# Expert products by pairs of tokens, and late columns through two output buffers, in a one-core decoder layer on Trainium2

## The reference, cut to what matters

```python
z = rms_norm(x) @ w_in                     # 38 column tiles of 128: 14 "z", 8 "conv", 16 "gate"
z = z + (token_shift(z) - z) * mu          # the 14 z tiles; the first mixer reads them
...
h = u * sigmoid(gate)                      # the 8 conv tiles, by pairs; the second mixer reads them
...
g = sigmoid(z_gate)                        # the 16 gate tiles
h = h + (g_r * o_r + g_c * o_c) @ w_out
# experts: 8 heads x 16 chosen rows = 128 rows of u_tab and 128 of v_tab for each token
coef = gates * gelu(einsum('cd,ced->ce', c, u_tab[idx]))
h = h + einsum('ce,ced->cd', coef, v_tab[idx])
...
```

## Time and profile before

| what | value |
|---|---|
| median of 3 runs | 3401.3 us (3399.88 to 3406.71) |
| the profiled execution | 3405.59 us |
| its span | 3403.9 us |
| granted TensorE clock over the span | 0.89 |
| TensorE busy | 2719.1 us (80%) |
| VectorE busy | 2378.7 us (70%) |
| GpSimd busy | 1978.4 us (58%) |
| ScalarE busy | 525.0 us (15%) |
| moved by DMA | 1248.57 MB, of them 1073.87 MB by the gathers |

### The profile page before, as it was taken

How to read it: one execution, slowest core, us unless ns; L and a number is a source line. 1 busy time by engine, 2 the same in 40 slices (tenths; PEclk the granted TensorE clock), 3 DMA queues, 4 the chain that set the end, 5 groups by cost and what they waited for, 6 DMA issues and landing times.

```text
span 3403.9 us, 41995 instructions
## 1 busy us (share of the span) xinstructions
PE 2719.1 (80%) x15556; PEld 1235.5 (36%) x15556; DVE 2378.7 (70%) x6051; ACT 525.0 (15%) x1166; POOL 1978.4 (58%) x2093
## 2 busy tenths in 40 slices
PE   9988985998989888897867687667766777777787
PEld 7877872333323233233323233232323331222111
DVE  5669898886677765777689877987798747665200
ACT  3221321110121101211010101010111001111101
POOL 1013344665656565566677667776767667666663
PEclk9998996998999999998878887798879788888899
DMA  6558998999999999999999999999999999999995
GB/s 212 197 181 301 334 364 286 373 399 380 371 352 385 390 364 362 340 406 390 410 409 403 405 401 409 397 407 405 400 396 408 406 404 410 409 388 406 410 369 235
DMA packets 385725, 1248.57 MB, mean 367 GB/s; under 512 B 40560, under 2 KB 75120, under 8 KB 384752
## 3 DMA queue, kind: packets, MB, share of 16 engines
q0 software_dynamic: 294912, 1073.87, 81.0%
q1 hardware_dynamic: 90608, 172.01, 14.1%
HBM read 1217.80 MB, written 27.92 MB: 366 GB/s over the span
## 4 chain that ended last, share of the span: by engine, by line
PE 34%; DMA 33%; DVE 16%; POOL 10%; issue 5%; ACT 1%; SPq 1%; POOLq 0%; ACTq 0%; DVEq 0%
DMA e_u<-in_u_tab,e_idx 12%; PE e_acc L1273 8%; DMA e_late<-in_u_tab,e_idx 7%; DMA e_v<-in_v_tab,e_idxT 6%; DVE e_u L2178 5%; PE e_pl L1361 5%; POOL e_v L949 4%; PE e_pd L1156 4%; POOL e_u L941 3%; PE e_acc L1318 3%; PE e_pd L1236 3%; PE e_acc L1343 3%; DVE e_late L2178 2%; PE e_pd L976 2%; DMA shifted_projection<-e_side 2%
## 5 line engine op out<-in xcount | busy, mean ns | idle before, releaser
L2178 DVE CUSTOM_DVE_ANT_0 e_u<-e_u,e_c 128x1024 f32<-128x1024 f32 x776 | 943.3, 1216 | 439.8 <-DMA e_u<-in_u_tab,e_idx 424.4
L941 POOL DMA_INDIRECT e_u<-in_u_tab,e_idx x776 | 757.7, 976 | 651.4 <-DVE e_dots L2178 260.2
L1273 PE MATMUL e_acc<-e_v,e_wd 128*32 128x512 f32 x3096 | 900.5, 675 | 284.5 <-DMA e_v<-in_v_tab,e_idxT 260.6
L949 POOL DMA_INDIRECT e_v<-in_v_tab,e_idxT x774 | 732.8, 947 | 434.7 <-PE e_acc L1273 279.2
L2178 DVE CUSTOM_DVE_ANT_0 e_late<-e_late,e_c 128x1024 f32<-128x1024 f32 x248 | 301.1, 1215 | 132.3 <-DMA e_late<-in_u_tab,e_idx 130.5
L1273 PEld LDWEIGHTS e_acc<-e_v,e_wd 128*32 128x32 f32 x3096 | 122.7, 113 | 736.6 <-DMA e_v<-in_v_tab,e_idxT 493.1
L1361 PE MATMUL e_pl<-e_late,e_v 128*128 128x512 f32 x608 | 342.0, 661 | 54.6 <-DVE e_late L1977 13.5
L1273 PE MATMUL e_acc<-e_late,e_wd 128*32 128x512 f32 x832 | 270.8, 712 | 105.0 <-DMA e_late<-in_v_tab,e_idxT 96.1
L941 POOL DMA_INDIRECT e_late<-in_u_tab,e_idx x248 | 240.5, 970 | 189.8 <-DVE e_dots L2178 148.9
L1906 DVE SCALAR_TENSOR_TENSOR e_gbc<-e_hc,e_cw,e_gbc 128x128 f32<-128x128 f32 x960 | 303.7, 343 | 0.5
L949 POOL DMA_INDIRECT e_late<-in_v_tab,e_idxT x208 | 198.2, 953 | 75.2 <-issue 53.1
(11 more groups left out here) (293 smaller groups left out, 3048.2 us busy)
## 6 DMA issues: line engine op xcount, KB each, us to landing
e_u<-in_w_in SPq DMA_DIRECT2D x38, 512.0 KB, 3.8
e_v<-in_w_in SPq DMA_DIRECT2D x38, 512.0 KB, 6.5
e_v<-in_w_in SPq DMA_DIRECT2D x76, 256.0 KB, 6.4
e_u<-in_u_tab,e_idx POOLq DMA_INDIRECT x776, 9.5
e_v<-in_v_tab,e_idxT POOLq DMA_INDIRECT x774, 9.5
e_zb<-in_w_c SPq DMA_DIRECT2D x48, 256.0 KB, 10.5
e_arena<-in_w_r SPq DMA_DIRECT2D x32, 256.0 KB, 19.8
e_zb<-in_w_r SPq DMA_DIRECT2D x32, 256.0 KB, 6.7
```

The source lines that it names most:

```text
L941: pool.indirect_dma_start(out=rows_in[i], out_offset=None, in_=io["u_tab"], in_offset=bass.IndirectOffsetOnAxis(ap=idx[n % 2][:, j:j + 1], ...
L949: pool.indirect_dma_start(out=rows_in[i], out_offset=None, in_=io["v_tab"], in_offset=bass.IndirectOffsetOnAxis(ap=idxT[n % (LAG + 1)][:, ...
L1273: last = pe.matmul(acc[rows, cols], w[:, at_:at_ + 32], rows_in[row][:, cols], start=(step == 0), stop=True, skip_group_check=True)
L2178: dve.tensor_tensor_reduce(rows_in[i], rows_in[i], c[:, :], 1.0, 0.0, ALU.mult, ALU.add, dots[n % 2][:, j:j + 1]).then_inc(s_dot, 1)
```

## The change

Three things are done. **Pairs:** ahead of MORE_AT the v products of tokens j - 1 and j are issued together in the odd slot, the first halves of both, then the second halves. From MORE_AT on it is one token in a slot as before, and after the last tile four together as before. **Two output buffers:** late columns write to `l_out[0]` and `l_out[1]` in turn, with a semaphore each; ScalarE waits for the store of the column before the previous one. A "conv gate" column uses the other buffer for its sigmoid and still waits for the previous store. **The z column:** ScalarE makes one pass over the bank in place of two (and the one element, now with the kept column as bias); the shifted part times mu is read by VectorE from the bank itself. The bank is now free after VectorE's step. In the diff the first `late_out` is ScalarE's and the second VectorE's.

```diff
             def late_store(m):
-                if kind(m) == "z":
-                    sp.wait_ge(s_lo, m + 1)
-                else:
-                    sp.wait_ge(s_lf, m + 1)
-                block_store(1, m, l_zo, s_lst)
+                sp.wait_ge(s_lf, m + 1)
+                o = stores_until(m)
+                block_store(1, m, l_out[o % 2], s_lst[o % 2])
...
-                    together = LAST_TOGETHER if t >= NT else TOGETHER
-                    if v_at(t, s) and s % together == 0:
-                        add_tokens(*v_at(t, s), together)
+                    if v_at(t, s):
+                        n, j = v_at(t, s)
+                        if t >= NT:
+                            if s % LAST_TOGETHER == 0:
+                                add_tokens(n, j, LAST_TOGETHER)
+                        elif t * SLOTS + s >= MORE_AT:
+                            add_tokens(n, j, 1)
+                        elif s % 2:
+                            add_tokens(n, j - 1, 2)
...
                 act.wait_ge(s_lu, CHUNKS * (m + 1))
-                i = stores_until(m)
+                o = stores_until(m)
+                out = l_out[o % 2]
...
-                else:
-                    act.wait_ge(s_lst, 16 * i)
+                if kind(m) == "conv gate":
+                    act.wait_ge(s_lst[(o + 1) % 2], 16 * ((o + 1) // 2))
+                    act.activation(l_out[(o + 1) % 2], pl[:, :], ACT.Sigmoid).then_inc(s_lf, 1)
+                elif o >= 2:
+                    act.wait_ge(s_lst[o % 2], 16 * (o // 2))
                 if kind(m) == "z":
-                    act.activation(l_zs[:, 0:1], col(z_last_b, column(m)), ACT.Copy)
-                    act.activation(l_zs[:, 1:], pl[:, :], ACT.Copy, scale=col(vec, COL["mu"] + column(m)))
-                    act.activation(l_zo, pl[:, :], ACT.Copy, scale=col(omm, column(m))).then_inc(s_lf, 1)
-                if kind(m) == "conv gate":
-                    act.activation(l_zs[:, 0:LATE_T], pl[:, :], ACT.Sigmoid).then_inc(s_lf, 1)
+                    act.activation(out[:, 0:1], pl[:, 0:1], ACT.Identity, scale=col(omm, column(m)), bias=col(z_last_b, column(m)))
+                    act.activation(out[:, 1:], pl[:, 1:], ACT.Copy, scale=col(omm, column(m))).then_inc(s_lo, 1)
                 if kind(m) == "gate":
-                    act.activation(l_zo, pl[:, :], ACT.Sigmoid).then_inc(s_lf, 1)
+                    act.activation(out, pl[:, :], ACT.Sigmoid).then_inc(s_lf, 1)
...
             def late_out(m):
+                o = stores_until(m)
+                out = l_out[o % 2]
                 if kind(m) == "z":
-                    dve.wait_ge(s_lf, m + 1)
-                    dve.tensor_tensor(l_zo, l_zs[:, 0:LATE_T], l_zo, ALU.add).then_inc(s_lo, 1)
+                    dve.wait_ge(s_lo, m + 1)
+                    dve.scalar_tensor_tensor(out=out[:, 1:], in0=pl[:, 0:LATE_T - 1], scalar=col(vec, COL["mu"] + column(m)),
+                                             in1=out[:, 1:], op0=ALU.mult, op1=ALU.add).then_inc(s_lf, 1)
                 else:
                     dve.wait_ge(s_lu, CHUNKS * (m + 1))
                     dve.wait_ge(s_lf, m)
-                    dve.tensor_tensor(l_zo, pl[:, :], l_zs[:, 0:LATE_T], ALU.mult).then_inc(s_lf, 1)
+                    if o >= 2:
+                        dve.wait_ge(s_lst[o % 2], 16 * (o // 2))
+                    dve.tensor_tensor(out, pl[:, :], l_out[(o + 1) % 2], ALU.mult).then_inc(s_lf, 1)
```

More of the change, by code:

```diff
@@ L501, in trunk @@
         x_second = [wd[k // (KT // 2)][:, k % (KT // 2) * P:(k % (KT // 2) + 1) * P] for k in range(KT)]
-        l_zs, l_zo = side[:, 0:LATE_T + 1], side[:, LATE_T + 1:2 * LATE_T + 1]
+        l_out = [side[:, i * 513:i * 513 + LATE_T] for i in range(2)]
         omm = buf("e_omm", [P, RWKV_TILES])
@@ L542, in trunk @@
         s_bx, s_bsq, s_bsum = sem("b_xT_in"), sem("b_x_squared"), sem("b_squares_summed")
[L543 removed]
+        s_bdve, s_bvar, s_brstd = sem("b_vector_step"), sem("b_variance_inverted"), sem("b_rstd_ready_then_second_tile_kept")
         s_lw, s_lu = [sem(f"l_w_in{i}") for i in range(CHUNKS)], sem("l_w_chunk_used")
[L545 removed]
+        s_lf, s_lo, s_lst = sem("l_output_ready"), sem("l_z_scaled"), [sem(f"l_output_stored{i}") for i in range(2)]
         s_aw, s_am = [sem(f"a_w_in{i}") for i in range(UW)], sem("a_column_tile_in_psum")
@@ L614, in stored @@
                 if b == 1:
-                    sp.wait_ge(s_lst, 16 * stores_until(m))
+                    for i in range(2):
+                        sp.wait_ge(s_lst[i], 16 * stores_until(m) // 2)
                 elif b is None and m <= FIRST_GATE:
@@ L687, in tail_loads @@
                     if m == 0:
-                        sp.wait_ge(s_lst, 16 * stores_until(COL_TILES))
+                        for i in range(2):
+                            sp.wait_ge(s_lst[i], 16 * stores_until(COL_TILES) // 2)
                     else:
```

9 lines of the change are left out of this document (3 added, 6 removed).

## The result

| kernel | median | ratio to before, 95% interval |
|---|---|---|
| before | 3399.9 us (3391.3 to 3406.7) | 1 |
| after | 3422.9 us (3418.2 to 3428.9) | 1.0068 (1.0050 to 1.0087) |

The account below looks back on a forecast made before the run. DMA gathers were taken to bound the kernel, so only DMA rest could be won: -13 - 8 + 5 + 2 = -14 us, with -3 for the low clock -17, giving a median of 3384 us; range 3360 to 3404.

Parts of the forecast that it names:

- Two output buffers: Late columns' stores: ScalarE's waits for the store just issued vanish and the holes behind them close; -13 us, bounds -16 and 0.
- z +2: Z columns: the bank comes free later, after VectorE's step in its queue, delaying v products; +2 us, bounds 0 and +10.
- Pairs on TensorE: V products before MORE_AT: a pair costs 0.98 us and not 1.96, so 154 pairs free 151 us of TensorE.
- Small pieces: DMA rest outside the named holes, 16 us: faster TensorE catch-up behind stalls wins half, -8 us, bounds -16 and 0.
- Pairs on the buffers: First row held for the second, slack 1.2 us of a turn: two late gathers in each of two mixer holes, +5 us.
- The ceiling: Period with late columns, 984 us: raising the DMA share from 0.98 to 1.02 can win at most 39 us.
- Low clock, -3: Late products behind avoided stalls: two of the 3.78 us rows return to 1.98 us; -3 us.
- Slower by held rows: Rival, every pair before MORE_AT: TensorE over 1.2 us late, waiting for the second row; +30 less 13, 3418 us; chance 0.14.
- The gain is given back: Rival: store holes close, but held rows and VectorE's place open as many; 3400 us; chance 0.20.
- signs of a wrong forecast: Next profile: longer v gather waits, DMA share 0.97 or less, holes at mixer's product and behind z columns, 3.78 us late products.
- products x8 in 1.05 us: Sign of a right forecast in the next profile: paired v products, eight records, take some 1.05 us.

Follow-up runs that it names:

- w1: The changed kernel with v products issued singly in their own slots, no pairs, run again as an anchor; 0.9929 of before.
- w4: The changed kernel without pairs, each single v product behind the late products of its own slot and not ahead of them; 1.0041 of before.
- w3: The changed kernel with each pair issued one slot earlier, in the even slot ahead of its late products; 0.9883 of before, 3363.6 us.
- w2: The changed kernel without pairs, with five v rows and three u rows between V_LAG and MORE_AT; 0.9929 of before.
- y3: The changed kernel, pairs kept, with five v rows and three u rows between V_LAG and MORE_AT; 0.9935 of before.
- y1: The changed kernel with a pair's two v products one behind the other in the odd slot, each waiting for its own row; 1.0064 of before.
- x2: The changed kernel without pairs: two output buffers and the new z column, v products singly in their own slots; 0.9938 of before.
- v1: The changed kernel with pairs in the even slot, and five v rows and three u rows between V_LAG and MORE_AT; 0.9919 of before.
- x1: The kernel before with the odd-slot pairs alone, late columns leaving as before; 1.0081 of before.
- y2: The changed kernel with GpSimd issuing both v gathers of a pair in the even slot, then the u gather; 1.0166 of before.
- z4: The changed kernel with pairs only in slots with none or one late product; 1.0099 of before, in the job where before took 3574 us.
- z2: The changed kernel with pairs in the even slot ahead of its late products; 1.0051 of before, in the job where before took 3574 us.

## Why the prediction was wrong

**The step that failed** is the one on the buffers: "Before: 0.3 + 7.7 + 1.05 = 9.1 us for a turn that has four slots, 12.8 us: 3.7 us are left for a TensorE that is elsewhere." With pairs it left 1.2 us, and priced them at +5. Of the 3.7 us 3.1 were not left, they were in use: so long a landed row stood on average until TensorE took it. Taken from the trace's landings as means over the v gathers of the 308 slots (landing, from the landing to the start of the product, the product, from its end to the next gather's start), the turn is

| kernel | landing | stands landed | product | to the next gather | turn | four slots |
|---|---|---|---|---|---|---|
| before | 8.0 | 3.1 | 1.1 | 0.6 | 12.8 | 12.8 |
| w1, columns only | 7.9 | 2.9 | 1.1 | 0.6 | 12.5 | 12.5 |
| w4, singles behind late products | 7.5 | 3.8 | 1.1 | 0.6 | 13.0 | 13.0 |
| after | 7.3 | 2.1 | 2.1 | 1.8 | 13.2 | 13.1 |
| w3, pairs in the even slot | 7.5 | 0.9 | 2.3 | 1.7 | 12.4 | 12.4 |

(for pairs the mean of both rows, and the product is the pair's, first record to last end: in after the even row stands 3.7 us and the odd one 0.5; in w3 2.5 and -0.7, since many pairs begin before their second row has landed). My 11.5 us with pairs followed the second row. Its way round in after is 3.0 us from the pair's end to its gather, 7.6 to land and 2.5 to the end of the next pair, where I had 2.8, 7.7 and 1.05 with 1.2 to spare. So the error lies with TensorE's part, 1.5 us more than the product alone; in w3 that last piece is 1.7 us.

A sign of it was there before the change: 189 of some 306 v gathers waited for a v product, the POOL row above. It is a sign and no proof, since w1 has as many such waits and a fifth buffer brings it nothing (w2). A longer hold is paid in part, and the faster landing gives the rest back: a buffer is out of service for 5.9 us of a turn in after and for 4.6 in w1 (all but the landing), the landing is 0.6 us shorter, and (1.3 - 0.6) / 4 x 308 = 54 us is what the rounded means give; the two periods differ by 1012 - 964 = 48. In w4, with nothing paired, it is 5.5 for 4.6 us of hold and 0.4 us of landing given back. In w3 the hold is 4.9 us, 0.3 more than in w1, and the landing is 0.4 us shorter: there the longer hold isn't paid.

These are accounts of where the turn went; why the landing is shorter by just so much they don't say. Nor does the mean number of gathers on their way decide alone (issue to landing, both tables): it is 5.1 in w1, 4.9 in w3 and 4.5 in after, but y3 keeps the DMA engines at 1.00 with 4.7 and y1 only at 0.97 with 4.8.

**Point by point.** *Two output buffers, -13 and z +2:* 21 to 24 us gained with singles (x2, w1); right in kind, too small. *Pairs on TensorE, 151 us set free:* the v products are busy 337.5 us for 1228 records before and 254.8 for 1232 after, so 83 us; by the row of rows 7, four strips in step, I took the best case for all. *Small pieces, -8:* not there in the changed kernel; in w3, where no product stands a slot late, the pairs bring 16 us against w1. That this gain comes from TensorE's saved time, as my -8 had it, isn't shown: with five v rows even pairs bring 0.1% (v1 against w2), within the intervals. *Pairs on the buffers, +5:* with the -8, the pairs' share of my sum was -3; measured +28 alone (x1) and +44 beside the columns. This is the error of the forecast. *The ceiling, 39 us:* w3 came to it (38.7 us by the medians, 30 by the profiled executions), with its share at 1.00 and not yet 1.02. The rounded shares allow 29 to 48 us and not 34 to 48; nothing hung on that. *Low clock, -3:* the two late products at 3.78 us behind store waits are gone, but the mean late product went from 661 to 681 ns, and the granted clock from 0.95 to 0.90: TensorE waits more. That this is no price is seen in y3, which at 0.92 is as fast as x2 at 0.95.

**The rivals.** "Slower by held rows", 3418, chance 0.14, is what came: 3423. Its condition, TensorE more than 1.2 us late for a pair, was narrowly met (1.5, above). That the sum came so near is in part luck: +30 stood for 44, -13 for -21. Its cause was half right: I put it on the wait for the second row, y1 and w4 put it on the place in TensorE's queue. "The gain is given back" had the right mechanism too and was too mild. What I named as signs of a wrong forecast was there: GpSimd's wait longer, a share of 0.97, holes at the mixer's product (849 to 861 at 0.63) and behind a column's end, more late products at the low level (63 of their 608 records last over 1 us, 30 before). The sign that should have been right, products x8 in 1.05 us, was 1.2 to 1.4 in dense slots.

**Packing and the bank, by page and by trace.** The Trainium skill, "TensorEngine Tiling (Array Packing)", Theoretical Speedup, gives up to four times for a dimension of 32 or less. An estimate from it is twice for a pair against two products that fill two strips each. The measured pair is 254.8 / 308 x 2 = 1.65 us of busy time against 2 x 1.10, a factor of 1.3: the trace stays well below the page's upper bound. The same page of the Trainium skill, PSUM Bottleneck, wants both ScalarE and VectorE to empty PSUM. Here the split, with two buffers for the z and conv columns, gained 0.2% beside singles and lost as much beside the odd pairs, each about as large as its interval; with it TensorE's wait for VectorE's step was 1.2 us a column and 3.0.

## What stays open

How much of y2's loss is the early odd row and how much the later u gather; z4's question, whether the thin slots carry all of the pairs' price; why the columns and the even pairs are no gain in the job with slower transfers; and where the even pairs' gain over singles comes from, since two singles in the even slot, or two products in the same strips, weren't run. Taking late products away to see the pair's wait alone wasn't tried.

## What to carry to other kernels

Before an instruction is moved later in its engine's queue, look at what it frees: if the trace shows a gather waiting for that very release in most of its turns, a delay is likely to be paid, even when the engine itself has time over (here a good half of it: 0.9 us more hold made a turn 0.5 us longer in w4, 1.3 us made it 0.7 longer in after). When two steps are to go together, try the place of the first, so that the compute engine waits for the second's data, before the place of the second, where the first's buffer waits; here this choice is the difference between +0.7% and -1.2%, on the level of 3400 us (on the level of 3574 the early place was +0.5%). What remains when known parts are subtracted from a turn is not yet slack: look in the trace how long the filled buffer stands, and take that off too.

## What the runs showed of the hardware that I had not expected

Two f32 v products, issued in a row into four different strips 32 columns wide, take no longer one behind the other than interleaved: two singles in a row (y1) are busy 241 us for some 1200 records, as interleaved pairs (246), where singles apart take 341 for 1248 (x2). No run put two products in a row into the same strips, so that it is the strips isn't shown. And the same kernel (w3 and z2) moved 405 GB/s in one job and 368 in another in 1700 to 3000 us, with the DMA share falling only from 1.02 to 0.98; the time of the kernel before went from 3402 to 3574 us between the two jobs.
